# Merge products of a four-branch decoder trunk: one fp32 product of two matmuls, or three passes over high and low parts

## The chip, the cores and the metric

The kernel runs on one core of a Trainium2 chip. The metric is the time of one execution on the device in microseconds (us), the median of three runs. In the text TensorE is PE (its weight loads PEld), VectorE is DVE, ScalarE is ACT, GpSimd is POOL and SyncE is SP, as in the profile.

## The reference, cut to what matters

Two layers. In each, the normalized activations `h` (512 tokens x 1024) meet one large input projection; its columns feed four mixers (A gated DeltaNet, "g" in the kernel; B latent attention, "m"; C RWKV-7, "r"; D top-k sparse attention, "d") and four gates of 1024 channels. Each mixer gives 256 features per token, which are projected to 1024, gated and summed:

```python
y_a = gdn_mixer(...)  @ w_out_gdn[l]      # (512 x 256) @ (256 x 1024)
y_b = mla_mixer(...)  @ w_out_mla[l]
y_c = rwkv7_mixer(...) @ w_out_rwkv[l]
y_d = dsa_mixer(...)  @ w_out_dsa[l]
merged = sigmoid(p_a) * y_a + sigmoid(p_b) * y_b + sigmoid(p_c) * y_c + sigmoid(p_d) * y_d
x = x + merged @ w_o[l]
hm = rms_norm(x, mlp_norm_g[l])
x = x + square(relu(hm @ w_up[l])) @ w_down[l]
```

Everything is float32. The change touches only the four `@ w_out` products.

## The kernel before, in words

Activations lie transposed: features on the 128 partitions, the 512 tokens along the free dimension. All large weight matrices are cut into units of 1024 x 128 (eight tiles of 128 x 128), 134 units a layer, streamed from one DRAM array in the order of `unit_list` (L59). A unit is loaded into one of three slots of `ring` by SP (L408 to L412, 512 KB). ACT then copies it into `w_hi` as fp32r, a reduced form of fp32 (`split_next`, L1178), and POOL subtracts to get the rest, `w_lo` (L446 to L452, two instructions of 128 x 512). `w_hi` and `w_lo` have two slots each, so a unit is split when the unit two before it has been consumed. The activations are held in the same two forms (`h_hi`, `h_lo`). PE makes the product in three passes, w_hi by h_hi, w_hi by h_lo, w_lo by h_hi: 24 matmuls of 128 x 512 a unit (`split_product`, L485, lines L491, L492 and L497).

A **merge unit** `("merge", br, i)` holds the gate weights of 128 of the 1024 channels of branch `br`, and behind them two tiles of 128 x 128 of that branch's outgoing matrix (128 KB). There are 32 a layer. PE makes the gate like any unit, into one of three PSUM banks that ACT empties (`bank_a`); ACT takes the sigmoid into one of four slots of `sg` and splits the next unit (`merge_sig`, L1147). `merge_outputs` (L561) then makes the outgoing product into one of four banks that DVE empties (`bank_v`): two plain fp32 matmuls, L567, whose operands are `out_ring` (the outgoing weights as loaded, six slots) and `yo` (the branch's 256 features, two slots of branches). The trace has two records for each fp32 matmul, so four for a product. DVE multiplies the product by the sigmoid and adds it to `mg` (`merge`, L1680: L1518 with output `sg`, then L1693; in branch 2, the first one, a single multiplication at L1689). Products are mostly made in pairs: two gates, then two products.

The order of every engine's work is written out by hand; each engine runs its own program in order, and semaphores join them. The order of a layer, with the branch numbers of the code (2 = RWKV, 0 = DeltaNet, 1 = latent attention, 3 = sparse attention):

1. Input projections and both recurrent mixers, with branch 2's merges between them. The RWKV features are made by DVE at L1889 and signalled by `r_out`; PE waits for it at L912, makes four products at once, then does two pairs (L930 and L938). Around there ACT takes two sets of inverse roots (L1354 and L1356), with table loads.
2. The DeltaNet features (L1940), then the projections of the sparse branch, then branch 0's eight merges (L985 to L1034), with the indexer's scores between them. DVE meanwhile adds up the scores (L1971) and runs a top-128 selection, cut into steps that `go_on` (L2004) takes from a generator: MAX8 (L1983), MATCH_REPLACE8 (L1985) and some steps behind them (L1989 to L1999).
3. Attention "m" (`attention`: L772 on PE, L1218 on ACT, L1697 on DVE). It works through 16 steps (4 query tiles x 4 heads), with the three first gates of branch 1 fed in as pieces (`gate_pieces`). ACT writes the attention's output into `yo` at L1237, eight pieces of 128 x 128, each one `m_y`.
4. Branch 1's merges: PE makes the fourth gate, waits for all eight `m_y` and makes four products, then two pairs. In the same stretch DVE runs the rest of the selection and the merges by turns (L2071 to L2079: attention, nine steps, two merges of two, eight steps, one merge, the last steps, one merge). Attention "d" needs the whole selection.
5. Attention "d" of the same form, branch 3's merges, then `wo`, `up` and `down`.

SP has one queue. For a merge unit it first loads the ring slot and then, behind a wait for `mg_done` (products merged by DVE), the outgoing weights (L413 to L417).

Of the kernel before, what the change touches and what calls it, by code (L numbers as in the profile page):

```python
# [16 lines left out]
ALU = mybir.AluOpType  # L17
ACT = mybir.ActivationFunctionType
F32 = mybir.dt.float32
# [25 lines left out]
INVERSE_STEPS = ("uc", "e", "x1", "ti", "y", "t", "x", "wt", "u")  # L45
# [7 lines left out]
OUT_RING = 6  # L53
# [113 lines left out]
def build(nc, x_in, pos_in, wstream, par_in, const_in, tabs, x_dram, out):  # L167
    ctx = ExitStack()
    with ctx:
        def sb(name, shape, dt=F32):  # L170
            return ctx.enter_context(nc.sbuf_tensor(name, shape, dt))
# [9 lines left out]
        out_ring = sb("out_ring", [P, OUT_RING, 2, P])  # L181
# [4 lines left out]
        yo = sb("yo", [P, 2, 2, T])  # L186
# [76 lines left out]
        for name, n in (  # L263
# [20 lines left out]
            ("m_ss", 16), ("m_p", 16), ("m_n", 16), ("m_pt", 16), ("m_y", 8),  # L284
            ("mg_sig", 32), ("mg_raw", 6), ("mg_done", 32), ("mg_hi", 8), ("mg_lo", 8), ("wo_done", 8), ("up_relu", 32), ("up_sq", 32), ("up_hi", 32), ("up_done", 32), ("g_zs", 1), ("r_s0", 1), ("g_s0", 1), ("down_done", 8 * QUARTERS),
# [54 lines left out]
        def merges_to(g):  # L340

            return sum(UNITS[i % NU][0] == "merge" for i in range(g))

        block = ctx.enter_context(nc.Block())
# [28 lines left out]
            tmp=ar(35, (T,)), ss=ar(11, (4, T)), pt=ar(15, (4, TT, P)),  # L373
# [4 lines left out]
            ss=ar(15, (4, T)), pt=ar(33, (4, TT, P)),  # L378
# [19 lines left out]
        def _(sp):  # L398
# [9 lines left out]
            for g in range(L * NU):  # L408
                l, u = divmod(g, NU)
                if g >= RING:  # L410
                    sp.wait_ge(S["split_lo"], g - RING + 1)
                sp.dma_start(ring[:, g % RING, :, :], wstream[g, :, 0:KT * P].rearrange("p (k n) -> p k n", n=P)).then_inc(w_here[g % RING], 16)  # L412
                if UNITS[u][0] == "merge":  # L413
                    n = merges_to(g)
                    if n >= OUT_RING:
                        sp.wait_ge(S["mg_done"], n - OUT_RING + 1)
                    sp.dma_start(out_ring[:, n % OUT_RING, :, :], wstream[g, :, KT * P:].rearrange("p (k n) -> p k n", n=P)).then_inc(out_here[n % OUT_RING], 16)  # L417
                if g == 0:
                    load_x(1)
                if g == 1:  # L420
                    sp.dma_start(consts[:, NFIRST:], const_in[:, NFIRST:]).then_inc(more_here, 16)
                if UNITS[u] == ("rw", 4):
                    if l == 0:
                        sp.wait_ge(S["x_t"], 8)
                    else:
                        sp.wait_ge(S["down_done"], at(l - 1, "down_done", 8 * QUARTERS))
                    sp.dma_start(x_dram, xT).then_inc(x_away, 16)
                if UNITS[u] == ("merge", 3, 0):
                    sp.wait_ge(S["m_y"], at(l, "m_y", 8))
                    sp.wait_ge(x_away, 16 * (l + 1))  # L430
                    sp.dma_start(xT, x_dram).then_inc(x_back, 16)
# [8 lines left out]
        def _(pool):  # L440
# [31 lines left out]
        def _(pe):  # L472
# [344 lines left out]
            for l in range(L):  # L817
# [94 lines left out]
                pe.wait_ge(S["r_out"], at(l, "r_out", 1))  # L912
# [72 lines left out]
                def indexed_merge(i):  # L985
                    numbers = []
                    for j in range(2):
                        numbers.append(gate(l, 0, 2 * i + j))
                        index_pair()
                    merge_outputs(1, numbers)  # L990
# [53 lines left out]
                pe.wait_ge(S["m_y"], at(l, "m_y", 8))  # L1044
# [10 lines left out]
                pe.wait_ge(S["d_y"], at(l, "d_y", 8))  # L1055
# [32 lines left out]
        def _(act):  # L1088
# [89 lines left out]
            def split_next():  # L1178


                g = units[0]
                if g < L * NU:
# [35 lines left out]
            def attention(l, x, V, slot, fill):  # L1218
                steps = [(qt, h) for qt in range(TT) for h in range(H)]
                for i in range(len(steps) + 3):  # L1220
# [12 lines left out]
                    if i >= 4 and i % 2 == 0:  # L1233
# [3 lines left out]
                        act_fn(yo[:, slot, h // 2, qt * P:(qt + 1) * P], b[:, 0:P], ACT.Copy).then_inc(S[x + "_y"], 1)  # L1237
# [33 lines left out]
            for l in range(L):  # L1271
# [173 lines left out]
                attention(l, "m", Mv, 0, lambda i: piecewise_sig(l, i))  # L1445
# [4 lines left out]
                attention(l, "d", Dv, 1, lambda i: piecewise_sig(l, i))  # L1450
# [50 lines left out]
        def _(dve):  # L1501
# [194 lines left out]

            def attention(l, x, V, scale, bias):  # L1697
                steps = [(qt, h) for qt in range(TT) for h in range(H)]
                scores = {}
                for i in range(len(steps) + 1):  # L1700
# [13 lines left out]
                    if i >= 1:  # L1714
# [5 lines left out]
                        v.tensor_scalar(e_, e_, att[:, 2, j % 4:j % 4 + 1], None, MUL).then_inc(S[x + "_n"], 1)  # L1720

# [35 lines left out]
            for l in range(L):  # L1757
# [472 lines left out]
```

## Time and profile before

| what | value |
|---|---|
| median of 3 runs | 2044.9 us (2044.44 to 2045.82) |
| the profiled execution's own time | 2043.76 us |
| its span | 2041.9 us |
| PE busy | 1987.6 us, 97% |
| DVE busy | 1087.1 us, 53% |
| ACT busy | 768.7 us, 38% |
| POOL busy | 737.3 us, 36% |
| granted TensorE clock, mean | 0.996 |

The span is the time from the first to the last instruction; the rest of the execution's time lies around it. A busy share is an average over the whole span. Each record of the trace belongs to a line of the kernel, and a helper's line stands for all its callers. Matmuls overlap, so that one's own duration is longer than the distance to the next; distances are read in the chain of waits, which goes back from the last instruction, at each step to what released it. What stands in square brackets behind an instruction of the timeline is the time its engine was idle before it, and what ended that.

### The profile page before, as it was taken

How to read it: one execution, taken by the hardware profiler on the slowest of the kernel's cores; microseconds unless marked ns; L12 is line 12 of the kernel's file. 1: busy time of each engine (PE TensorE's matmuls, PEld its weight loads, DVE VectorE, ACT ScalarE, POOL GpSimd, SP SyncE). 2: the span in 40 equal slices, each digit the busy share in tenths (PEclk: the TensorE clock that was granted, in tenths of full speed). 3: DMA queues.
4: the chain of work that ended last, by engine and by line, in shares of the span. 5: the costliest groups of instructions: out<-in, count | busy, mean ns of one | idle time of the engine just before them, and what ended most of it. 6: DMA issues, size and time to landing. Idle time of an engine off the chain costs nothing.

```text
span 2041.9 us, 31745 instructions
## 1 busy us (share of the span) xinstructions
PE 1987.6 (97%) x13120; PEld 1526.7 (75%) x13120; DVE 1087.1 (53%) x1807; ACT 768.7 (38%) x1206; POOL 737.3 (36%) x553
## 2 busy tenths in 40 slices
PE   6999999999999999999999999999999999999997
PEld 5788787756667888888867877776566778888886
DVE  8785555896833422222487756379876343222223
ACT  5442523344353442322354353234344433332323
POOL 3431313422324444444444132243213344444442
PEclk9999999999999999999999999999999999999999
DMA  6220112211312332333332111123122223233332
GB/s 231 75 81 28 57 34 78 84 59 50 122 55 77 114 102 93 95 101 93 97 121 90 47 37 58 43 79 95 52 78 81 68 85 101 93 101 95 94 102 73
DMA packets 51647, 169.42 MB, mean 83 GB/s; under 512 B 5728, under 2 KB 14048, under 8 KB 50864
## 3 DMA queue, kind: packets, MB, share of 16 engines
q1 hardware_dynamic: 50448, 163.11, 24.9%
q0 software_dynamic: 1056, 4.28, 0.6%
q8 instruction: 105, 1.72, 0.3%
q14 instruction: 38, 0.31, 0.0%
HBM read 160.29 MB, written 7.08 MB: 82 GB/s over the span
## 4 chain that ended last, share of the span: by engine, by line
PE 84%; DVE 11%; ACT 3%; issue 1%; DMA 0%; POOL 0%; ACTq 0%; SPq 0%; DVEq 0%
PE bank_a L491 13%; PE bank_a L497 13%; PE bank_a L492 13%; PE bank_v L497 7%; PE bank_v L491 7%; PE bank_v L492 7%; PE bank_v L567 4%; PE bank_v L645 3%; DVE arena L1518 1%; PE bank_a L804 1%; PE bank_f L599 1%; PE bank_f L605 1%; PE bank_f L578 1%; DVE mg L1524 1%; PE bank_a L793 1%
## 5 line engine op out<-in xcount | busy, mean ns | idle before, releaser
L451 POOL TENSOR_TENSOR w_lo<-ring,w_hi 128x512 fp32r<-128x512 f32 x536 | 729.6, 1382 | 1207.4 <-ACT w_hi L1184 1207.2
L491 PE MATMUL bank_a<-h_hi,w_hi 128*128 128x512 f32 x1296 | 523.8, 404 | 3.9 <-DVE h_lo L1557 3.9
L492 PE MATMUL bank_a<-h_lo,w_hi 128*128 128x512 f32 x1296 | 505.7, 390 | 0.0
L1184 ACT ACTIVATE w_hi<-ring 128x1024 fp32r<-128x1024 f32 x268 | 281.5, 1050 | 222.6 <-DVE arena L2118 212.4
L497 PE MATMUL bank_a<-h_hi,w_lo 128*128 128x512 f32 x1296 | 321.4, 390 | 0.0
L491 PEld LDWEIGHTS bank_a<-h_hi,w_hi 128*128 128x128 f32 x1296 | 243.4, 188 | 75.0 <-issue 19.4
L492 PEld LDWEIGHTS bank_a<-h_lo,w_hi 128*128 128x128 f32 x1296 | 243.6, 188 | 57.1 <-issue 8.1
L497 PEld LDWEIGHTS bank_a<-h_hi,w_lo 128*128 128x128 f32 x1296 | 244.0, 188 | 50.8
L491 PE MATMUL bank_v<-parts,w_hi 128*128 128x512 f32 x640 | 251.3, 393 | 1.4 <-DVE parts L2087 1.4
L492 PE MATMUL bank_v<-parts,w_hi 128*128 128x512 f32 x640 | 249.1, 389 | 0.0
L1518 DVE TENSOR_TENSOR sg<-bank_v,sg 128x512 f32<-128x512 f32 x112 | 77.4, 691 | 310.5 <-PE bank_v L497 239.3
L2106 DVE TENSOR_TENSOR arena<-arena 128x512 f32<-128x512 f32 x64 | 44.3, 692 | 244.7 <-ACT arena L1477 244.7
L497 PE MATMUL bank_v<-parts,w_lo 128*128 128x512 f32 x640 | 158.1, 389 | 0.0
L491 PEld LDWEIGHTS bank_v<-parts,w_hi 128*128 128x128 f32 x640 | 120.1, 188 | 29.0 <-DVE parts L2087 4.1
L497 PEld LDWEIGHTS bank_v<-parts,w_lo 128*128 128x128 f32 x640 | 120.1, 188 | 25.0
L492 PEld LDWEIGHTS bank_v<-parts,w_hi 128*128 128x128 f32 x640 | 120.2, 188 | 24.9 <-issue 0.5
L1477 ACT ACTIVATE arena<-bank_a 128x512 f32<-128x512 f32 x64 | 38.3, 598 | 205.6 <-PE bank_a L497 205.6
L567 PE MATMUL bank_v<-yo,out_ring 128*128 128x512 f32 x256 | 114.7, 594 | 0.0
L1154 ACT ACTIVATE sg<-bank_a 128x512 f32<-128x512 f32 x52 | 31.1, 597 | 202.1 <-PE bank_a L497 202.1
L1518 DVE TENSOR_TENSOR arena<-arena 128x512 f32<-128x512 f32 (+3 forms) x77 | 97.8, 1270 | 10.7 <-ACT arena L1247 8.2
L567 PEld LDWEIGHTS bank_v<-yo,out_ring 128*128 128x128 f32 x256 | 48.0, 189 | 54.5 <-issue 53.0
L645 PE MATMUL bank_v<-arena 64*64 64x64 f32 x2176 | 66.2, 219 | 3.1 <-ACT arena L1107 2.1
(296 smaller groups left out, 2505.5 us busy)
## 6 DMA issues: line engine op xcount, KB each, us to landing
ring<-in_w SPq DMA_DIRECT2D x268, 512.0 KB, 3.5
out_ring<-in_w SPq DMA_DIRECT2D x64, 128.0 KB, 3.4
x_dram<-arena SPq DMA_DIRECT2D x2, 2048.0 KB, 8.8
arena<-x_dram SPq DMA_DIRECT2D x2, 2048.0 KB, 9.1
arena<-in_x SPq DMA_DIRECT2D x2, 1024.0 KB, 9.4
out_x<-arena SPq DMA_DIRECT2D x4, 512.0 KB, 3.7
consts<-in_const SPq DMA_DIRECT2D x1, 1189.0 KB, 13.6
arena<-tabs POOLq DMA_DIRECT2D x2, 512.0 KB, 3.9
```

Source lines behind the costliest of these rows:

```text
L451: ins = nc.gpsimd.tensor_tensor(w_lo[:, g % SPLIT, ks, :], raw, w_hi[:, g % SPLIT, ks, :].bitcast(F32), ALU.subtract)
L491: mm(b[:], w_hi[:, s, k, :], hi[:, k, :], start=k == 0, stop=False)
L492: mm(b[:], w_hi[:, s, k, :], lo[:, k, :], start=False, stop=False)
L497: ins = mm(b[:], w_lo[:, s, k, :], hi[:, k, :], start=False, stop=k == KT - 1)
L567: ins = mm(b[:], out_ring[:, n % OUT_RING, k, :], yo[:, slot, k, :], start=k == 0, stop=k == 1)
L578: mm(b[:], hi[:, k, :], h_hi[:, k, :], start=k == 0, stop=False)
L645: ins = mm(b[quarter(p_), k * C:(k + 1) * C], lhs[quarter(p_), m, :], rhs(m, p_), start=True, stop=True)
L1154: act_fn(sg[:, n % GATES, :], b[:], ACT.Sigmoid).then_inc(S["mg_sig"], 1)
L1184: act_fn(w_hi[:, g % SPLIT, :, :], ring[:, g % RING, :, :], ACT.Copy).then_inc(S["split_hi"], 1)
L1477: act_fn(relu[:, n % 2, :], b[:], ACT.Relu).then_inc(S["up_relu"], 1)
L1518: link(v.tensor_tensor(out_, a, b, op))
L2106: v.tensor_tensor(relu2[:, n % 2, :], relu[:, n % 2, :], relu[:, n % 2, :], MUL).then_inc(S["up_sq"], 1)
```

## The change

The product of the outgoing weights becomes three passes over high and low parts, as for all other weights.

- **PE**, `merge_outputs`: six fp32r matmuls of 128 x 512 in place of two fp32 matmuls; it waits for `ow_lo` instead of the load.
- **Weights.** `out_ring`, `out_hi` and `out_lo` have four slots where `out_ring` had six. `out_ring` and `out_lo` share their bytes (the `with` block gives its space back, and `out_lo` is allocated next), so POOL subtracts in place, and a slot is loaded anew only when the product from it has been merged. For each pair of merge units, SP loads the outgoing weights of both at the unit behind the second gate, ACT makes two `out_hi` (128 x 256 each) and POOL two `out_lo` (128 x 256 each), each ahead of its own part of that unit's split. That split is done when the pair's first gate has been consumed. `outgoing(g)` gives the pair for unit g.
- **Features.** `yo` gives way to `y_hi` and `y_lo` of one branch. For r and g, DVE writes the features to the arena and then parts them, two copies and two subtractions of 128 x 512 (`parts_of`). In the attentions ACT copies each piece twice, into `y_hi` and into `yt`, and DVE subtracts in four instructions of 128 x 256 (`low_rows`), three inside the loop, from step 8, and one behind it.
- **Waits.** PE waits for `r_yl`, `g_yl`, `m_yl`, `d_yl` where it waited for the features. DVE waits in `low_rows` for ACT's `m_y` and `d_y`.

```diff
-OUT_RING = 6
+OUT_RING = 4
...
-        out_ring = sb("out_ring", [P, OUT_RING, 2, P])
+        out_hi = sb("out_hi", [P, OUT_RING, 2, P], F32R)
+        with nc.sbuf_tensor("out_ring", [P, OUT_RING, 2, P], F32) as out_ring:
+            pass
+        out_lo = sb("out_lo", [P, OUT_RING, 2, P], F32R)
...
+        def outgoing(g):
+
+            if not 0 < g < L * NU or UNITS[(g - 1) % NU][0] != "merge" or merges_to(g - 1) % 2 == 0:
+                return []
+            second = merges_to(g - 1)
+            first_owner = max(i for i in range(g - 1) if UNITS[i % NU][0] == "merge")
+            return [(second - 1, first_owner), (second, g - 1)]
...
-                if UNITS[u][0] == "merge":
-                    n = merges_to(g)
+                for n, owner in outgoing(g):
                     if n >= OUT_RING:
                         sp.wait_ge(S["mg_done"], n - OUT_RING + 1)
-                    sp.dma_start(out_ring[:, n % OUT_RING, :, :], wstream[g, :, KT * P:]...
+                    sp.dma_start(out_ring[:, n % OUT_RING, :, :], wstream[owner, :, KT * P:]...
...
+                for n, owner in outgoing(g):
+                    pool.wait_ge(S["ow_hi"], n + 1)
+                    slot = n % OUT_RING
+                    nc.gpsimd.tensor_tensor(out_lo[:, slot, :, :], out_ring[:, slot, :, :], out_hi[:, slot, :, :].bitcast(F32), ALU.subtract).then_inc(S["ow_lo"], 1)
                 pool.wait_ge(S["split_hi"], g + 1)
...
-                    pe.wait_ge(out_here[n % OUT_RING], 16 * (n // OUT_RING + 1))
+                    pe.wait_ge(S["ow_lo"], n + 1)
+                    hi, lo = out_hi[:, n % OUT_RING], out_lo[:, n % OUT_RING]
                     for k in range(2):
-                        ins = mm(b[:], out_ring[:, n % OUT_RING, k, :], yo[:, slot, k, :], start=k == 0, stop=k == 1)
+                        mm(b[:], hi[:, k, :], y_hi[:, k, :], start=k == 0, stop=False)
+                        mm(b[:], hi[:, k, :], y_lo[:, k, :], start=False, stop=False)
+                    for k in range(2):
+                        ins = mm(b[:], lo[:, k, :], y_hi[:, k, :], start=False, stop=k == 1)
...
                 g = units[0]
+                for n, owner in outgoing(g):
+                    if n >= OUT_RING:
+                        act.wait_ge(S["mg_done"], n - OUT_RING + 1)
+                    act.wait_ge(out_here[n % OUT_RING], 16 * (n // OUT_RING + 1))
+                    act_fn(out_hi[:, n % OUT_RING, :, :], out_ring[:, n % OUT_RING, :, :], ACT.Copy).then_inc(S["ow_hi"], 1)
...
-                        act_fn(yo[:, slot, h // 2, qt * P:(qt + 1) * P], b[:, 0:P], ACT.Copy).then_inc(S[x + "_y"], 1)
+                        rows = slice(qt * P, (qt + 1) * P)
+                        act_fn(y_hi[:, h // 2, rows], b[:, 0:P], ACT.Copy)
+                        act_fn(V["yt"][:, h // 2, rows], b[:, 0:P], ACT.Copy).then_inc(S[x + "_y"], 1)
...
+            def parts_of(l, x, src):
+
+                for f in range(2):
+                    link(v.tensor_copy(y_hi[:, f, :], src[:, f, :]))
+                    v.tensor_tensor(y_lo[:, f, :], src[:, f, :], y_hi[:, f, :].bitcast(F32), SUB).then_inc(S[x + "_yl"], 1)
+
+            def low_rows(l, x, V, qt):
+
+                rows = slice(qt * P, (qt + 1) * P)
+                dve.wait_ge(S[x + "_y"], at(l, x + "_y", 2 * qt + 2))
+                v.tensor_tensor(y_lo[:, :, rows], V["yt"][:, :, rows], y_hi[:, :, rows].bitcast(F32), SUB).then_inc(S[x + "_yl"], 1)
...
+                    if i >= 8 and i % 4 == 0:
+                        low_rows(l, x, V, i // 4 - 2)
+                low_rows(l, x, V, TT - 1)
...
-                v.tensor_tensor(yo[:, 0, :, :], R["o"], R["g"], MUL).then_inc(S["r_out"], 1)
+                v.tensor_tensor(R["o"], R["o"], R["g"], MUL).then_inc(S["r_out"], 1)
                 dve.wait_ge(S["r_out"], reached("r_out"))
+                parts_of(l, "r", R["o"])
...
-                v.tensor_tensor(yo[:, 1, :, :], G["o"], G["z"], MUL).then_inc(S["g_out"], 1)
+                v.tensor_tensor(G["o"], G["o"], G["z"], MUL).then_inc(S["g_out"], 1)
                 dve.wait_ge(S["g_out"], reached("g_out"))
+                parts_of(l, "g", G["o"])
```

## Rows read from the trace of the kernel before

**Rows 1.** The page, part 4: the chain of waits by engine.
```profile
PE 84%; DVE 11%; ACT 3%; issue 1%; DMA 0%; POOL 0%; ACTq 0%; SPq 0%; DVEq 0%
```

**Rows 2.** Chain of waits behind attention d: start, us, what.
```profile
604.52 1.81 PE bank_a L497 x8
609.96 1.81 PE bank_a L497 x8
611.77 3.43 PE bank_v L567 x8
...
626.13 1.73 PE bank_v L567 x4
627.89 0.70 DVE sg L1518
```

**Rows 3.** Stretches (start:end, length; PE, PEld, DVE, ACT, POOL busy; clock, DMA).
```profile
376.00:471.00 95.00, 95.00 (x345) 58.49 (x343) 89.46 (x164) 35.86 (x53) 28.75 (x21) 1.00 0.23 72
471.00:509.00 38.00, 35.61 (x215) 25.00 (x216) 21.36 (x74) 19.97 (x59) 5.08 (x5) 1.00 0.16 50
509.00:552.00 43.00, 43.00 (x168) 29.62 (x164) 39.24 (x66) 13.67 (x18) 16.35 (x12) 1.00 0.37 128
```

**Rows 4.** Timeline of DVE in branch 0's merges.
```profile
396.49 2.87 DVE L1971 SCALAR_TENSOR_TENSOR arena<-arena,ab 128x384 f32<-128x384 f32 x2 [0.26 <-ACT arena L1396]
...
403.00 2.87 DVE L1971 SCALAR_TENSOR_TENSOR arena<-arena,ab 128x384 f32<-128x384 f32 x2 [0.22 <-ACT arena L1396]
...
414.11 0.43 DVE L1518 TENSOR_TENSOR arena<-arena 128x256 f32<-128x256 f32 x1
...
429.10 3.03 DVE L1971 SCALAR_TENSOR_TENSOR arena<-arena,ab 128x512 f32<-128x512 f32 x2 [0.41 <-ACT arena L1396]
```

**Rows 5.** DVE and POOL together, and DVE alone.
```profile
462.54 2.98 POOL L451 TENSOR_TENSOR w_lo<-ring,w_hi 128x512 fp32r<-128x512 f32 x2 [24.27 <-ACT w_hi L1184]
...
464.41 1.66 DVE L2068 TENSOR_TENSOR arena<-arena 32x512 f32<-32x512 f32 x1
...
467.54 0.68 DVE L2068 TENSOR_TENSOR arena<-arena 32x512 f32<-32x512 f32 x1
```

**Rows 6.** Timeline of DVE behind attention m, layer 0, and the same wait in layer 1.
```profile
503.68 0.41 DVE L1521 TENSOR_SCALAR arena<-arena,m 128x384 f32<-128x384 f32 x1
...
517.39 0.69 DVE L1518 TENSOR_TENSOR sg<-bank_v,sg 128x512 f32<-128x512 f32 x1
...
548.99 0.69 DVE L1518 TENSOR_TENSOR sg<-bank_v,sg 128x512 f32<-128x512 f32 x1 [2.02 <-PE bank_v L567]
...
552.38 0.29 DVE L1711 CUSTOM_DVE_ANT_0 arena<-bank_v,consts 128x128 f32<-128x128 f32 x1
...
1506.15 0.41 DVE L1521 TENSOR_SCALAR arena<-arena,m 128x384 f32<-128x384 f32 x1
...
1551.47 0.69 DVE L1518 TENSOR_TENSOR sg<-bank_v,sg 128x512 f32<-128x512 f32 x1 [2.01 <-PE bank_v L567]
```

**Rows 7.** Timeline of ACT in attention m and its end, layer 0 and layer 1.
```profile
481.29 0.28 ACT L1237 ACTIVATE yo<-bank_a 128x128 f32<-128x128 f32 x1 [0.62 <-PE bank_a L804]
481.47 0.59 ACT L1165 ACTIVATE sg<-bank_f 128x512 f32<-128x512 f32 x1
...
509.41 0.28 ACT L1237 ACTIVATE yo<-bank_a 128x128 f32<-128x128 f32 x1 [2.29 <-PE bank_a L804]
...
1511.89 0.28 ACT L1237 ACTIVATE yo<-bank_a 128x128 f32<-128x128 f32 x1 [2.29 <-PE bank_a L804]
```

**Rows 8.** Timeline of PE in attention m.
```profile
482.20 0.47 PE L599 MATMUL bank_f<-h_hi,w_hi 128*128 128x512 f32 x1 [0.58 <-ACT sg L1165]
```

**Rows 9.** Chain of waits around the RWKV features.
```profile
209.57 0.94 ACT w_hi L1184
210.53 1.28 ACT L1245
211.83 0.70 ACT arena L1245
212.57 1.13 PE bank_a L770 x2
```

**Rows 10.** Groups of ACT by shape: busy, mean ns; idle before.
```profile
L1184 ACT ACTIVATE w_hi<-ring 128x1024 fp32r<-128x1024 f32 x268 | 281.5, 1050 | 222.6 <-DVE arena L2118 212.4 <-PE bank_v L848 10.1
L1216 ACT ACTIVATE h_hi<-mg 128x512 fp32r<-128x512 f32 x16 | 9.7, 626 | 0.4
```

**Rows 11.** Timeline of ACT between the DeltaNet's pair matrices.
```profile
255.35 1.09 ACT L1120 ACTIVATE arena<-bank_a 128x512 f32<-128x512 f32 x2 [0.19 <-PE bank_a L620]
```

**Rows 12.** Timeline of DVE behind the RWKV features and the DeltaNet features.
```profile
220.99 0.69 DVE L1689 TENSOR_TENSOR mg<-bank_v,sg 128x512 f32<-128x512 f32 x1 [4.93 <-PE bank_v L567]
...
336.70 0.69 DVE L1518 TENSOR_TENSOR arena<-bank_v,arena 128x512 f32<-128x512 f32 x1 [0.58 <-PE bank_v L970]
...
343.05 0.69 DVE L1518 TENSOR_TENSOR arena<-bank_v,arena 128x512 f32<-128x512 f32 x1 [2.12 <-PE bank_v L970]
```

**Rows 13.** The page, part 6: issues, KB each, us to landing.
```profile
out_ring<-in_w SPq DMA_DIRECT2D x64, 128.0 KB, 3.4
```

More of the change, by code:

```diff
@@ L44 @@
 BLOCK = 8
-INVERSE_STEPS = ("uc", "e", "x1", "ti", "y", "t", "x", "wt", "u")
+INVERSE_STEPS = ("yl", "uc", "e", "x1", "ti", "y", "t", "x", "wt", "u")
 GDN0, MLA0, RWK0, DSA0, GATE0 = 0, 1032, 1448, 2472, 3824
@@ L185, in build @@
         par = sb("par", [P, NPAR])
-        yo = sb("yo", [P, 2, 2, T])
+        y_hi = sb("y_hi", [P, 2, T], F32R)
+        y_lo = sb("y_lo", [P, 2, T], F32R)
         misc = sb("misc", [P, 2, T])
@@ L284, in build @@
             ("m_ss", 16), ("m_p", 16), ("m_n", 16), ("m_pt", 16), ("m_y", 8),
+            ("r_yl", 2), ("g_yl", 2), ("m_yl", 4), ("d_yl", 4), ("ow_hi", 32), ("ow_lo", 32),
             ("mg_sig", 32), ("mg_raw", 6), ("mg_done", 32), ("mg_hi", 8), ("mg_lo", 8), ("wo_done", 8), ("up_relu", 32), ("up_sq", 32), ("up_hi", 32), ("up_done", 32), ("g_zs", 1), ("r_s0", 1), ("g_s0", 1), ("down_done", 8 * QUARTERS),
@@ L372, in build @@
             iq=ar(15, (4, T)), q=ar(19, (2, T)), k=ar(21, (2, T)), vf=ar(23, (2, T)), v=ar(25, (TT, 256)), tab=ar(27, (2, T)), ik=ar(29, (T,)),
-            tmp=ar(35, (T,)), ss=ar(11, (4, T)), pt=ar(15, (4, TT, P)),
+            tmp=ar(35, (T,)), ss=ar(11, (4, T)), pt=ar(15, (4, TT, P)), yt=ar(27, (2, T)),
         )
@@ L377, in build @@
             tab=ar(27, (2, T)), tmp=ar(29, (T,)), bias=ar(32, (T,)), kr=ar(33, (T,)),
-            ss=ar(15, (4, T)), pt=ar(33, (4, TT, P)),
+            ss=ar(15, (4, T)), pt=ar(33, (4, TT, P)), yt=ar(27, (2, T)),
         )
@@ L911, in _ @@
                 more.append(gate(l, 2, 3))
-                pe.wait_ge(S["r_out"], at(l, "r_out", 1))
+                pe.wait_ge(S["r_yl"], at(l, "r_yl", 2))
                 merge_outputs(0, numbers)
@@ L989, in indexed_merge @@
                         index_pair()
+                    pe.wait_ge(S["g_yl"], at(l, "g_yl", 2))
                     merge_outputs(1, numbers)
@@ L1043, in _ @@
                 numbers.append(gate(l, 1, 3))
-                pe.wait_ge(S["m_y"], at(l, "m_y", 8))
+                pe.wait_ge(S["m_yl"], at(l, "m_yl", 4))
                 merge_outputs(0, numbers)
@@ L1054, in _ @@
                 numbers.append(gate(l, 3, 3))
-                pe.wait_ge(S["d_y"], at(l, "d_y", 8))
+                pe.wait_ge(S["d_yl"], at(l, "d_yl", 4))
                 merge_outputs(1, numbers)
@@ L1216, in norm_root, with attention @@
                         act_fn(h_hi[:, k, :], mg[:, k, :], ACT.Copy).then_inc(S["n_hi"], 1)
-            def attention(l, x, V, slot, fill):
+            def attention(l, x, V, fill):
                 steps = [(qt, h) for qt in range(TT) for h in range(H)]
@@ L1444, in _ @@
                 merge_sig(l)
-                attention(l, "m", Mv, 0, lambda i: piecewise_sig(l, i))
+                attention(l, "m", Mv, lambda i: piecewise_sig(l, i))
                 late_sig(l, 3)
@@ L1449, in _ @@
                 merge_sig(l)
-                attention(l, "d", Dv, 1, lambda i: piecewise_sig(l, i))
+                attention(l, "d", Dv, lambda i: piecewise_sig(l, i))
                 late_sig(l, 6)
```

2 lines of the change are left out of this document (1 added, 1 removed).

## The prediction

> **What bounds the kernel now.** I read the busy shares first: PE is at 97%, and that is an average. The chain of waits gives the ends: 84% PE, 11% DVE, 3% ACT [rows 1]. So a microsecond off PE is a microsecond off the time only where the chain runs through PE. Three stretches decide this change, and for them I read the stretches' busy times and then each engine's timeline.
>
> In branch 0's merges, from 376 us to the start of attention m, PE is busy for the whole 95 us, but DVE is too, 89.5 of 95 [rows 3]; what is missing is mostly the small gaps between its short instructions. DVE waits for other work only three times behind the first product, 0.26, 0.22 and 0.41 us, 0.89 together [rows 4]. From 429 us to 472 us it doesn't wait at all, and the next attention starts when it is through. In attention m DVE has room (21.4 of 38 us) and PE leads (35.6) [rows 3]. In branch 1's merges PE is again busy throughout and DVE 39.2 of 43 [rows 3]: DVE starts on the selection at 503.68, and its only wait before attention d is 2.02 us, for the first product of the last pair [rows 6]. Layer 1 shows the same 2.01. Behind attention d, and around branch 2, PE leads.
>
> **What a product gains.** A unit of 24 fp32r matmuls comes every 5.44 us (604.52 to 609.96), and eight of them take 1.81 us, so one takes 0.227 us [rows 2]. Two fp32 products take 3.43 us, one 1.717 [rows 2]. Six fp32r matmuls take 6 x 0.227 = 1.36 us. PE is relieved of 0.357 us a product, 22.8 us over 64. Bounds for the new matmul: the same kind of operands and the same changing of weights in each unit gives 0.227; the nearest dearer row is half an fp32 matmul, 0.429, which would make the product dearer than before. I take 0.227, since `split_product` has the same three passes.
>
> **Branch 2 (per layer).** Eight products on the path give 8 x 0.357 = 2.86 us. Two costs stand against it. ACT makes two `out_hi` ahead of a `w_hi`. No row shows a copy of 128 x 256 into fp32r; 128 x 1024 takes 1.05 us and 128 x 512 0.63 [rows 10], so the straight line gives 0.41, and the next instruction begins some 0.1 us before an end (0.94 in the chain for 1.05) [rows 9, 10]: 0.32 each, 0.65 a pair. Bounds are 0.43 (half of 0.63 less the overlap, twice) and 1.06 (0.63 less the overlap, twice). The pair of gates 2 and 3 falls at 209.57, where the chain runs through ACT: w_hi, table load, logarithm, then PE's matmuls that wait for its bank [rows 9]. That is +0.65 in full. The pair of gates 6 and 7 falls ahead of the copies at 255.35, where ACT had waited only 0.19 for PE [rows 11], and PE waits for these copies' banks: +0.46. Net 1.75 us gained. The parting of the features by DVE (two copies, two subtractions; 0.69 us or less each by the 128 x 512 rows, 2.8 together) is hidden: DVE idled 4.93 us ahead of the first product it merges [rows 12], and PE reaches `r_yl` later than DVE does. Without that cover it would be 2.8. The same for g lies ahead of waits of 0.58 and 2.12 us [rows 12], and its products come 50 us later: nothing, 0.1 us if only the first two waits counted.
>
> **Branch 0.** Eight products, but DVE leads: of 2.86 us only its own waits can go, 0.89. Late next is DVE itself. Here POOL's new work counts: four pairs, two subtractions of 128 x 256 each. Half of POOL's 2.98 for two of 128 x 512 is 1.49 for one [rows 5], so about 0.75 for a new one, 1.5 a pair. Beside POOL a DVE instruction with two inputs in SBUF takes 1.66 us instead of 0.68, 0.98 more for a POOL instruction of 1.49 [rows 5]; for one of 0.75 that is 0.5, or 1.0 a pair. Bounds: 0 if all fall on other instructions (half of DVE's work there is MAX8 and MATCH_REPLACE8), 4.0 for all four. I take 1.5, since two pairs fall on the rotary and elementwise parts. Net 0.6 us lost.
>
> The Trainium skill, "SBUF — State Buffer", section "Who interferes with whom", says that a VectorE instruction with two SBUF inputs contends with a GpSimd one that reads SBUF, and that the later one is blocked until the other ends. By the rows above the trace agrees. It is the rule that speaks against this change, and the dear end below is it at its worst.
>
> **Attentions m and d.** ACT copies each output piece twice; the second copy moves what is behind it by 0.18 us (481.29 to 481.47) [rows 7]. Twice in an attention what stands behind is the emptying of `bank_f`, for which PE waits (0.58 us) [rows 7, 8]: 0.36 us. The first pair's `out_hi` (0.65) delays an exponential whose result PE needs two steps later; DVE's three `low_rows` in the loop (0.43 each by the 128 x 256 row [rows 4]) fall into its idle time. Bounds 0 and 8 x 0.18 + 0.65 = 2.1 each; I take 0.5 each, 1.0 together.
>
> **Behind attention m: the term that decides.** The last `low_rows` of attention m waits for all eight pieces, and stands on DVE ahead of the rest of the selection. DVE was through with the attention at 503.68, the last piece is begun by ACT at 509.41 [rows 6, 7]. With the second copy it is there at 509.41 + 0.18 + 0.28 = 509.87; 0.43 for the subtraction, and DVE goes on at 510.3, 6.6 us later. Queued behind it are all selection steps and the eight merges of branch 1, and attention d waits for these. DVE had 2.02 us of idle time to take this up [rows 6], so attention d starts 4.6 us later, and the PE time of branch 1's eight products gives nothing, since PE then has to wait for DVE. Layer 1 has the same distance, 1511.89 to 1506.15 [rows 6, 7].
>
> The load of the third pair now waits until 18 products are merged. DVE starts merging at 517.39 + 6.6 = 524.0 [rows 6] and has two done by about 527.9; 3.4 us to landing [rows 13], 0.65 on ACT and about 1.4 on POOL let PE start that pair at 533.4, some 2 us late. The last pair is then ready before 550, and DVE comes for it at 553.6: hidden, by 4 us. Behind attention d the same wait of DVE costs nothing, because it has only merges to do there.
>
> **Branch 3.** PE leads: seven products give 2.5 us; the last is covered by DVE, which needs longer for a product than PE (it begins to merge at 627.89, and the second product isn't on the chain [rows 2]). 2.4 us with a little lost at the end.
>
> **Sum per layer:** -1.75 (branch 2), +0.6 (branch 0), +1.0 (attentions), +4.6 (wait behind attention m), -2.4 (branch 3) = +2.05; over two layers +4.1 us. The profiled execution took 2043.76 us (2.0 less in the span), so it would take 2047.9; the median of the runs is 1.1 above it, so the forecast is 2049.0.
>
> **Rivals.**
> - *Faster: DVE's wait is covered.* If DVE had more than 6.6 us idle between the attentions, the wait would vanish, and its 2.02 us could be gained as well: per layer -1.75 + 0.6 + 1.0 - 2.0 - 2.4 = -4.6, together -9.1, 2035.8 us. For it: PE is busy there without a gap. Against it: 2.02 us is all that the timeline shows.
> - *No difference that counts: the small costs hide.* ACT's copies and POOL's subtractions find room: -2.86 - 0.89 + 4.6 - 2.5 = -1.65 a layer, 2041.6 us. For it: ACT is busy for 20 of 38 us in the attention and POOL for 5 [rows 3].
> - *Clearly slower: the new POOL and ACT work falls on DVE's and PE's path.* All four pairs of branch 0 at 1.0 instead of 1.5 in all (+2.5), and each attention 0.8 dearer (+1.6): +4.1 a layer more, 2057 us. It decides from two-input DVE instructions beside every pair on. For it: rows 5. Against it: much of DVE's work there has one input.
> - *The passes aren't at 0.227 us.* Then PE gains nothing or loses. Nothing in the trace speaks for it.
>
> **How the numbers follow.** Forecast 0.50, covered wait 0.13, small costs hidden 0.17, POOL and ACT dear 0.17, passes dear 0.03. What a measurement of this kernel can tell from no change is about 0.2%, 4.1 us, so from 2040.8 to 2049.0 counts as the same. The forecast sits on that edge and is halved. Slower: 0.25 + 0.17 + 0.03 = 0.45. Same: 0.25 + 0.14 = 0.39. Faster: 0.13 + 0.03 = 0.16. The range, 2041 to 2057, holds the forecast, the hidden and the dear case; the forecast's own is 2045 to 2053.
>
> **What would show it.** Six records of 0.227 us distance a product. DVE idle for about 5.7 us ahead of its first instruction behind attention m, released by ACT's copy, and no wait left before attention d, which starts some 4.6 us later relative to attention m's end. The stretch from branch 0's first product to attention m as long as before or slightly longer. `up` and `down` unchanged. The forecast is wrong if DVE resumes the selection near the time it did, if attention d starts earlier, or if PE waits for `ow_lo` pair by pair.

## The result, and the profile after

| | before | after |
|---|---|---|
| median | 2043.86 us (20 runs) | 2047.25 us (20 runs) |
| profiled execution, its span | 2043.76, 2041.9 us | 2047.01, 2045.2 us |
| granted clock of that execution, mean | 0.996 | 0.992 |

The ratio is 1.0018, with a 95% interval of 1.0011 to 1.0025: 3.7 us more, clear of the noise, and just inside what the prediction counted as no difference. The medians are 3.4 us apart. One of the 20 executions of after took 10981.48 us; it is left out of the ratio, and without it the median is 2047.01. The forecast was 2049.0.

The page of after, parts 1 and 4: PE has 15 us less to do, POOL 55 and ACT 25 more, and part of the chain that ended last has moved from PE (84% [rows 1], now 76%) to DVE (11%, now 19%).

```profile
PE 1972.5 (96%) x13248; PEld 1553.6 (76%) x13248; DVE 1109.9 (54%) x1839; ACT 794.2 (39%) x1302; POOL 792.8 (39%) x617
...
PE 76%; DVE 19%; ACT 3%; issue 1%; DMA 0%; POOL 0%; ACTq 0%; SPq 0%; DVEq 0%
```

The chain of waits of after in branch 3, which answers to [rows 2] (start, us, what). A product is six distances of 0.23, 1.40 us in all (613.06 less 611.66), where it was 1.72.

```profile
609.85 1.81 PE bank_a L513 x8
611.66 0.23 PE bank_v L584
611.89 0.23 PE bank_v L585
612.13 0.23 PE bank_v L584
612.36 0.23 PE bank_v L585
612.59 0.47 PE bank_v L587 x2
613.06 0.23 PE bank_v L584
```

DVE's timeline of after behind attention m, layer 0 and 1, for [rows 6]. The subtraction waits for ACT; the selection follows at 506.28, where DVE began at 503.68 although attention m now ended 4 us earlier. In front of attention d there is no wait left.

```profile
499.89 0.42 DVE L1735 TENSOR_TENSOR y_lo<-arena,y_hi 128x256 fp32r<-128x256 f32 x1
505.94 0.42 DVE L1735 TENSOR_TENSOR y_lo<-arena,y_hi 128x256 fp32r<-128x256 f32 x1 [5.63 <-ACT arena L1265]
506.28 0.41 DVE L1549 TENSOR_SCALAR arena<-arena,m 128x384 f32<-128x384 f32 x1
...
549.21 0.69 DVE L1546 TENSOR_TENSOR sg<-bank_v,sg 128x512 f32<-128x512 f32 x1
...
552.11 0.29 DVE L1751 CUSTOM_DVE_ANT_0 arena<-bank_v,consts 128x128 f32<-128x128 f32 x1
...
1512.19 0.43 DVE L1735 TENSOR_TENSOR y_lo<-arena,y_hi 128x256 fp32r<-128x256 f32 x1 [5.63 <-ACT arena L1265]
```

PE's timeline of after, at the end of the same stretch and ahead of layer 1's inverse roots: what DVE lost is now PE's idle time.

```profile
552.23 0.55 PE L804 MATMUL bank_v<-arena 64*128 64x128 f32 x1 [6.59 <-DVE mg L1721]
...
1214.92 2.07 PE L790 MATMUL bank_a<-arena,consts 128*128 128x512 f32 x2 [2.26 <-ACT arena L1273]
```

Stretches of after, columns as in [rows 3], the granted clock third from the end. Behind either idle time it falls; in the kernel before it is 1.00 in the same places.

```profile
548.00:550.00 2.00, 0.00 (x0) 0.00 (x0) 1.87 (x4) 0.00 (x0) 0.00 (x0) 0.78 0.22 88
550.00:552.00 2.00, 0.00 (x0) 0.00 (x0) 1.93 (x3) 0.00 (x0) 0.00 (x0) 0.50 0.14 36
552.00:554.00 2.00, 1.19 (x6) 0.96 (x7) 1.55 (x12) 1.18 (x5) 0.00 (x0) 0.50 0.32 99
554.00:556.00 2.00, 2.00 (x7) 1.51 (x6) 0.68 (x5) 0.80 (x5) 0.00 (x0) 0.52 0.00 0
...
1212.00:1216.00 4.00, 1.74 (x4) 0.56 (x3) 3.93 (x3) 3.97 (x5) 4.00 (x3) 0.84 0.08 28
1216.00:1220.00 4.00, 4.00 (x14) 2.84 (x13) 3.92 (x5) 2.96 (x4) 1.77 (x2) 0.74 0.00 0
```

Where the time went, from the same instruction's start in both traces (after less before). Layer 0 opens 1.01 us ahead at the RWKV features, which is not the change: in the trace of before the clock fell to 0.50 at 44 us, behind 2.26 us of idle time of PE, and in the trace of after it did not, behind the same 2.26 (before, then after).

```profile
44.00:48.00 4.00, 3.83 (x10) 2.86 (x11) 3.76 (x9) 0.00 (x0) 0.00 (x0) 0.57 0.39 131
...
44.00:48.00 4.00, 3.68 (x16) 2.85 (x16) 3.77 (x8) 0.48 (x1) 0.00 (x0) 1.00 0.37 131
```

| stretch | forecast | layer 0 | layer 1 |
|---|---|---|---|
| branch 2 | -1.75 | -1.95 | -0.4 |
| branch 0 | +0.6 | -1.35 | -1.0 |
| attention m | +0.5 | +0.35 | +2.0 |
| wait and branch 1 | +4.6 | +3.7 | +3.7 |
| attention d | +0.5 | +1.45 | } -0.2 |
| branch 3 | -2.4 | -1.95 | } |
| sum | +2.05 | +0.25 | +4.1 |

### The profile page after: what moved, and what is told of

It is laid out like the page before. It is cut to its first block, busy times and chain, and to the rows that moved or that the text cites. A ratio compares the mean times of both kernels' runs of the same rounds, so it can differ in the third digit from the quotient of the medians.

```text
span 2045.2 us, 32253 instructions
## 1 busy us (share of the span) xinstructions
PE 1972.5 (96%) x13248; PEld 1553.6 (76%) x13248; DVE 1109.9 (54%) x1839; ACT 794.2 (39%) x1302; POOL 792.8 (39%) x617
## 3 DMA queue, kind: packets, MB, share of 16 engines
q8 instruction: 106, 1.74, 0.3%
## 4 chain that ended last, share of the span: by engine, by line
PE 76%; DVE 19%; ACT 3%; issue 1%; DMA 0%; POOL 0%; ACTq 0%; SPq 0%; DVEq 0%
PE bank_a L507 11%; PE bank_a L513 11%; PE bank_a L508 11%; PE bank_v L513 7%; PE bank_v L507 7%; PE bank_v L508 7%; PE bank_v L665 3%; DVE arena L2030 3%; DVE m L2028 3%; DVE arena L1546 2%; DVE arena L2016 2%; DVE mg L1721 1%; DVE sg L1546 1%; PE bank_f L619 1%; PE bank_a L824 1%
## 5 line engine op out<-in xcount | busy, mean ns | idle before, releaser
L507 PEld LDWEIGHTS bank_a<-h_hi,w_hi 128*128 128x128 f32 x1296 | 243.6, 188 | 72.7 <-issue 16.7
L462 POOL TENSOR_TENSOR out_lo<-out_ring,out_hi 128x256 fp32r<-128x256 f32 x64 | 55.7, 890 | 297.5 <-ACT out_hi L1207 297.5
L665 PEld LDWEIGHTS bank_v<-arena 64*64 64x64 f32 x2176 | 64.9, 135 | 3.5 <-ACT arena L1128 2.8
```

The lines of the kernel that those rows point to most:

```text
L462: nc.gpsimd.tensor_tensor(out_lo[:, slot, :, :], out_ring[:, slot, :, :], out_hi[:, slot, :, :].bitcast(F32), ALU.subtract).then_inc(S["ow ...
L507: mm(b[:], w_hi[:, s, k, :], hi[:, k, :], start=k == 0, stop=False)
L665: ins = mm(b[quarter(p_), k * C:(k + 1) * C], lhs[quarter(p_), m, :], rhs(m, p_), start=True, stop=True)
```

## The experiments

Each was timed in five rounds beside the kernel before. The first four shared a chip (before: 2043.24 us there), so did the next four (2043.87) and the last two (2043.04). Between groups, and against the changed kernel, the ratios to before are the safer comparison; differences of medians are given with them. A trace is of one execution, which can lie some us from the median. `before_wait` and `before_steps` start from the kernel before, the others from the changed kernel.

### low_split: the last subtraction behind four selection steps

```diff
-                low_rows(l, x, V, TT - 1)
+                if x != "m":
+                    low_rows(l, x, V, TT - 1)
...
-                go_on(9)
+                go_on(4)
+                low_rows(l, "m", Mv, TT - 1)
+                go_on(5)
```

> The changed kernel, with one thing moved: attention m's last low_rows (the subtraction that waits for ACT's last copy) stands behind four steps of the selection instead of ahead of them. Theory (the wait in front of the queued selection costs 3.7 us a layer by the trace, and PE's idle 6.6 us ahead of attention d another 1 us by a clock of 0.5 behind it): DVE starts on the selection without a wait, its wait for ACT shrinks to under 1 us, the next attention starts some 4 to 5 us earlier in each layer, and the time falls by 8 to 10 us against the changed kernel, to 2037 to 2039 us, 5 to 7 us under the kernel before. Rival (the wait is covered by other idle time, and what the change costs is ACT's and POOL's new work): within 2 us of the changed kernel, about 2047 us.

2036.14 us, ratio to before 0.9968 (0.9957 to 0.9979): 11.1 us under the changed kernel by the medians, 10.2 by the two ratios, at or a little above the upper end of what was expected, and the sign of the whole change turns. DVE's timeline:

```profile
498.96 0.42 DVE L1735 TENSOR_TENSOR y_lo<-arena,y_hi 128x256 fp32r<-128x256 f32 x1
499.29 0.41 DVE L1549 TENSOR_SCALAR arena<-arena,m 128x384 f32<-128x384 f32 x1
...
505.41 0.43 DVE L1735 TENSOR_TENSOR y_lo<-arena,y_hi 128x256 fp32r<-128x256 f32 x1
```

The subtraction comes behind the fourth step and waits for nothing. Attention d starts at 546.77 instead of 552.11; 1.0 us of this was there before branch 0, and 4.4 are the move. In layer 1 the two traces move 6.1 us apart, 1.6 of them because the clock did not fall at attention m's start this time. DVE still has no wait in branch 1, and PE idles ahead of attention d: DVE is the bound of this stretch now.

```profile
546.88 0.34 PE L804 MATMUL bank_v<-arena 64*128 64x128 f32 x1 [2.19 <-DVE mg L1721]
```

### before_wait: the wait alone, in the kernel before

```diff
                 attention(l, "m", Mv, 96 ** -0.5, lambda qt: Mv["bias"][:, (3 - qt) * P:T])
+                dve.wait_ge(S["m_y"], at(l, "m_y", 8))
```

> The kernel before, with one wait added: DVE waits for the eighth m_y (ACT's last copy of attention m) ahead of the selection. Nothing else of the change is in it. Theory (this wait alone costs, in any kernel with this order): DVE resumes 6.0 to 6.1 us later (509.41 + 0.28 against 503.68), 2.0 of it is taken up by its idle time, so 4 us a layer, and up to 1 us for the clock behind PE's new idle time: 2052 to 2054 us. Rival (the wait is hidden, and the changed kernel's loss comes from its other new work): 2044 to 2045 us, as the kernel before.

2058.61 us, ratio 1.0073 (1.0060 to 1.0086): 15.4 us (15 by the ratio), half as much again as expected. The mechanism stands, its price was too low. DVE's timeline shows the wait as expected, and behind it two instructions of 0.62 and 0.56 us (128 x 384) that take 1.74 and 1.54:

```profile
509.13 0.42 DVE L1521 TENSOR_SCALAR arena<-arena,m 128x384 f32<-128x384 f32 x1 [5.96 <-ACT yo L1237]
509.59 0.96 DVE L1994 TENSOR_TENSOR_SCAN arena<-arena 128x384 f32<-128x384 f32 x1
510.59 1.74 DVE L1524 SCALAR_TENSOR_TENSOR arena<-arena,sml 128x384 f32<-128x384 f32 x1
512.36 1.54 DVE L1518 TENSOR_TENSOR arena<-arena 128x384 f32<-128x384 f32 x1
```

Moved by 6 us, the selection's two-input steps meet POOL's subtractions. By the offsets of the two traces in layer 0 the wait costs 6.0 us, these two 2.1, the steps up to 545.58 another 0.7, and 3.4 are taken up before attention d (2.0 of them DVE's old idle time), so that attention d starts 5.4 late, in layer 1 too. Attention d itself is 2.2 us longer in layer 0 and 1.7 in layer 1, with the clock at 0.50 behind PE's 5.71 us of idle time; that term was expected at 1 us at most. Together this is 14.6 us. Another 1.4 us lie in layer 1's recurrent stretch, ahead of the wait, and have no cause shown here.

### two_pass: the third pass left out

```diff
-                        mm(b[:], hi[:, k, :], y_lo[:, k, :], start=False, stop=False)
-                    for k in range(2):
-                        ins = mm(b[:], lo[:, k, :], y_hi[:, k, :], start=False, stop=k == 1)
+                        ins = mm(b[:], hi[:, k, :], y_lo[:, k, :], start=False, stop=k == 1)
```

> The changed kernel without the third pass of the outgoing product (low part of the weights by high part of the features is left out of the result): four matmuls of 0.234 us instead of six. All weights are still loaded and parted and all waits are kept. Theory (PE's time per product counts in branches 2 and 3 alone, where PE leads; in branch 0 and branch 1 DVE leads): 15 products a layer by 0.47 us, 7.0 us a layer, 14 us in all, to 2033 us, with at most 2 us more. Rival (PE's time counts in all 32 products of a layer): 30 us, to 2017 us. Rival (the passes hide in other waits): under 5 us.

2036.53 us, ratio 0.9963 (0.9949 to 0.9976): 10.7 us under the changed kernel by the medians, 10.2 by the ratios: less than the 14, or 12 at the least, of the theory, and far from 30. In layer 0, branches 2 and 3 give 2.5 and 2.3 us behind their first product and 0.5 for that one, 5.8 together. Branch 1 gives 0.6 us a layer and branch 0 nothing: the trace is 0.53 us ahead of the changed kernel's behind the last merges of branch 2, and 0.31 behind it at the start of attention m. What is missing goes along with the clock. PE now idles 2.47 us inside branch 0 (0.48 in the changed kernel) and 2.06 ahead of attention m (1.17); the clock fell behind the first in both layers and behind the second in layer 0, and the execution's mean clock is 0.988. In this kernel relieving PE where DVE leads bought idle time, and a lower clock came with it.

### low_split_roots: the pair's copies behind the inverse roots

```diff
-                for n, owner in outgoing(g):
-                    ...
+                if g >= L * NU or UNITS[g % NU] != ("merge", 2, 4):
+                    outgoing_hi(g)
...
                 inverse_roots(G["rs"], ...)
+                outgoing_hi(l * NU + UNITS.index(("merge", 2, 4)))
```

> The changed kernel with the last low_rows of attention m moved as in low_split, and the two out_hi of branch 2's second pair made behind the inverse roots of the DeltaNet instead of ahead of w_hi. Theory (two copies of 0.61 us in all stand on the chain ahead of the roots, and in layer 1 they lengthen PE's idle time from 1.65 to 2.26 us, behind which the clock falls): 0.5 us a layer and about 1 us of clock in layer 1, so 1.5 to 2.5 us under low_split. Rival (PE is the bound there and catches up, or the copies come just as late for POOL and PE): within 0.5 us of low_split.

2036.53 us, ratio 0.9962 (0.9950 to 0.9975), no difference from low_split. Yet PE's idle time at the roots went back from 2.27 to 1.66 us and the clock stayed at 1.00 there in both layers. In layer 1 DVE's first merge came at 1218.79, 1.1 us ahead of low_split; behind the start of attention m this was gone, where the clock fell (0.74 and 0.83 between 1466 and 1474) behind 1.17 us of idle time. In low_split the same idle time had left it at 1.00. Inconclusive by itself, so it was repeated on a better base below.

### steps_inside: selection steps into attention m's idle time

```diff
-                go_on(9)
+                go_on(8)
...
-                attention(l, "m", Mv, 96 ** -0.5, lambda qt: Mv["bias"][:, (3 - qt) * P:T])
-                go_on(4)
-                low_rows(l, "m", Mv, TT - 1)
-                go_on(5)
+                attention(l, "m", Mv, 96 ** -0.5, lambda qt: Mv["bias"][:, (3 - qt) * P:T],
+                          lambda i: go_on(1) if i in (8, 12, 14) else None)
+                go_on(2)
+                low_rows(l, "m", Mv, TT - 1)
+                go_on(7)
```

> low_split with three selection steps moved into attention m, where DVE has idle time (3.2, 2.7 and 3.3 us ahead of the scores of steps 8, 12 and 14): one of the nine in front of attention m and two from behind it. Theory (since the change DVE is the bound in branch 0 and branch 1, and PE's idle time ahead of an attention, 1.18 us for m and 2.19 us for d, costs itself and then a fallen clock): attention m starts 1.2 us earlier, attention d another 2.2 us, and the clock behind attention d's start stays at 1.00 (0.8 us more): 3.4 to 4.2 us a layer, to 2028 to 2030 us. Rival (DVE's steps delay attention m itself, or PE becomes the bound at once): 0 to 2 us in all, 2034 to 2036 us.

2033.11 us (2029.61 to 2037.08), ratio 0.9951 (0.9939 to 0.9963): 3 us under low_split (3.5 by the ratios) where 6 to 8 were expected. The trace is of an execution of 2036.69 us, in which the clock fell at layer 0's roots, at layer 1's attention m and at both attentions d. The moved steps cost attention m nothing, but two of them had covered ACT: DVE waits 2.79 us for the last copy again. PE's rows ahead of the attentions:

```profile
468.42 0.46 PE L804 MATMUL bank_v<-arena 96*128 96x128 f32 x2 [1.18 <-DVE mg L1721]
...
547.88 0.34 PE L804 MATMUL bank_v<-arena 64*128 64x128 f32 x1 [1.26 <-DVE mg L1721]
```

1.18 us ahead of attention m is what it was, though the last pair's first merge came 1.1 us earlier than in low_split and attention m started 0.7 us earlier. PE makes a product in 1.40 us and DVE merges one in 1.45 at best, so at the end of a pair DVE still has a merge to do, and PE waits for the bank. Here the additions to `mg` took 1.28 and 0.93 us, beside POOL, where 0.69 is the undisturbed time: 0.83 of the 1.18 us. That this is the whole of it is argued and not tested. The expectation that this idle time would go was wrong.

### steps_inside_roots

The two edits together.

> steps_inside, with the two out_hi of branch 2's second pair behind the inverse roots, as in low_split_roots, which gained nothing over low_split: at the roots the clock stayed at 1.00 in both layers, but it fell at the start of attention m in layer 1 behind 1.17 us of idle time. Theory (the gain at the roots was real, 0.5 us and once 1 us of clock, and was lost to that fall): with no idle time ahead of attention m it shows, 1 to 2 us under steps_inside. Rival (the copies only change place): within 0.5 us of steps_inside.

2031.10 us, ratio 0.9937 (0.9925 to 0.9948), 2.0 us under steps_inside as the theory had it. The intervals of the two ratios overlap, and the executions of steps_inside alone lie 7.5 us apart, so it is likely and not settled.

### busy_pe: useless work for PE

```diff
-                    for k in range(2):
-                        ...
+                    for _ in range(1 + again * (n == numbers[-1])):
+                        ...
...
-                    merge(l, 1, 0, i)
+                    merge(l, 1, 0, i, again=i == 3)
```

> low_split with useless work: in branch 1 the last product's six matmuls are done twice in each layer (1.4 us more for PE), in the 2.19 us in which PE idles ahead of attention d. Theory (the clock falls behind an idle time of 2.17 us and more, and did not behind 1.65 us or less ahead of the roots): PE's idle time is 0.8 us, the clock stays at 1.00 at attention d's start, and the kernel becomes 0.8 to 0.9 us a layer shorter through more work, 2034.5 us. Rival (the fall has another cause, or the repeat delays DVE's last merge, for which it has 0.9 us to spare): equal to low_split or up to 1 us a layer longer.

2035.58 us, ratio 0.9963 (0.9950 to 0.9975), 0.6 us under low_split (1.0 by the ratios) and within its interval. PE idles 0.76 us instead of 2.19; in layer 1 the clock stayed at 1.00, in layer 0 it fell to 0.66 all the same. Inconclusive.

### double_pool: POOL's new work twice

```diff
                 pool.wait_ge(S["split_hi"], g + 1)
+                for n, owner in outgoing(g):
+                    nc.gpsimd.tensor_tensor(w_lo[:, g % SPLIT, 0:2, :], ring[:, g % RING, 0:2, :], w_hi[:, g % SPLIT, 0:2, :].bitcast(F32), ALU.subtract).then_inc(S["ow_lo"], 1)
+                    pool.wait_ge(S["ow_lo"], 4 * (n // 2) + 3 + n % 2)
```

> low_split with POOL's new work doubled: for each outgoing weight tile POOL subtracts another 128 x 256 (0.9 us), behind out_lo, into the part of w_lo that its next instruction writes. This doubles what the change put on POOL beside DVE, and delays w_lo by 1.8 us at 16 units a layer. Theory (POOL's subtractions cost DVE little, since most of DVE's work beside them has one input): under 1 us a layer, 2036 to 2038 us. Rival (each of the POOL subtractions holds a two-input DVE instruction of the selection stretch or of a merge; where DVE leads, seven pairs a layer by 0.5 to 1.0 us): 3.5 to 7 us a layer, 2043 to 2050 us.

2039.09 us, ratio 0.9979 (0.9970 to 0.9987): 3.0 us over low_split by the medians, 2.2 by the ratios, whose intervals overlap: 1.1 to 1.5 a layer, between the two expectations. POOL's and DVE's timelines in front of attention m:

```profile
457.94 2.33 POOL L465 TENSOR_TENSOR w_lo<-ring,w_hi 128x256 fp32r<-128x256 f32 x2
460.34 6.35 POOL L470 TENSOR_TENSOR w_lo<-ring,w_hi 128x512 fp32r<-128x512 f32 x4
```

```profile
460.43 1.75 DVE L1549 TENSOR_TENSOR arena<-arena 32x512 f32<-32x512 f32 x1
462.21 1.66 DVE L2117 TENSOR_TENSOR arena<-arena 32x512 f32<-32x512 f32 x1
```

DVE runs the same 164 instructions in layer 0 from 376 us of before to the start of attention m. Their durations add up to 90.65 us in the kernel before, 89.86 in the changed one, 89.88 in low_split and 90.72 here; the idle time between them is 5.57, 5.03, 5.03 and 5.42 us. Layer 1 has the same order (91.16, 90.34, 90.26, 91.23). So the change's own pairs cost DVE nothing in sum, since other instructions than before met POOL, and doubling them cost 0.8 us and 0.4 of idle time. The rest of the loss isn't the lock alone: behind 1.76 us of idle time ahead of attention m, 1.18 in low_split, the clock fell in both layers here and in neither there, 1.6 us each, and branch 1 gave 1.0 of them back.

### best, and before_steps

`best` is steps_inside_roots with the wait covered:

```diff
-                go_on(2)
+                go_on(4)
                 low_rows(l, "m", Mv, TT - 1)
-                go_on(7)
+                go_on(5)
```

> steps_inside_roots with attention m's last low_rows behind four selection steps instead of two. There DVE waited 2.79 us for ACT's last copy, and PE idled 1.26 us ahead of attention d. Theory (what DVE loses there ahead of attention d comes back until the last product of branch 1 decides): DVE's wait goes, PE idles 0.8 us or less ahead of attention d, 0.5 to 1.3 us a layer, to 2029 to 2030 us. Rival (PE is the bound there already, and the 1.26 us are DVE's merge behind the last product): within 0.5 us of 2031.1.

2030.59 us (2028.08 to 2031.39), ratio 0.9935 (0.9923 to 0.9948). DVE's wait for ACT is gone, and it waits for the product instead:

```profile
541.48 0.69 DVE L1552 TENSOR_TENSOR sg<-bank_v,sg 128x512 f32<-128x512 f32 x1 [3.55 <-PE bank_v L587]
```

PE is the bound of branch 1 again. The 2.79 us brought 0.5 by the medians and nothing that can be told by the ratios (0.9935 and 0.9937), the rival's answer: they had been covered. PE still idles 0.99 us ahead of attention d. The trace is of the fastest of the five executions, and its chain has less DVE than before the change [rows 1]:

```profile
PE 88%; DVE 7%; ACT 3%; issue 1%; DMA 0%; POOL 0%; ACTq 0%; SPq 0%; DVEq 0%
```

This is the lowest median, 12.5 us under the kernel before and 16.7 under the changed one; from steps_inside_roots it can't be told apart.

`before_steps` puts the same three steps inside attention m of the kernel before.

> The kernel before, with the same three selection steps inside attention m as in steps_inside (one from in front, two from behind), and nothing else. Theory (before the change PE is busy without a gap in branch 0 and branch 1, so earlier selection steps give nothing; they pay only once the three passes have made DVE the bound): 2042 to 2044.5 us, no difference that can be measured. Rival (the selection steps pay in any kernel, and the change isn't needed for it): 3 to 6 us faster, 2038 to 2041 us.

2043.29 us, ratio 1.0000 (0.9991 to 1.0009). So `best` isn't a better order of the selection with the change thrown in: without the three passes these steps give nothing, and the three passes as first placed cost 3.7 us.

## Why the prediction was right, point by point

**The deciding term** was forecast from two rows and held: DVE resumes 6.55 us later relative to the attention's end, 6.6 forecast. low_split removes it and the gain appears; before_wait adds it alone and the loss appears. 3.7 us a layer instead of 4.6 reached attention d, because DVE and POOL met less in sum: the 75 instructions of DVE from its return to the selection up to attention d took 0.86 us less than before. Three at the start took 1.7 us more; of those that took less, two in the last steps of the selection (before, then after):

```profile
543.88 1.67 DVE L1518 TENSOR_TENSOR arena<-arena 128x512 f32<-128x512 f32 x1
545.58 1.40 DVE L1998 TENSOR_SCALAR arena<-arena 128x512 f32<-128x512 f32 x1
...
548.02 0.69 DVE L1546 TENSOR_TENSOR arena<-arena 128x512 f32<-128x512 f32 x1
548.75 0.43 DVE L2043 TENSOR_SCALAR arena<-arena 128x512 f32<-128x512 f32 x1
```

In before_wait the same 75 took 1.33 us more. A wait's price depends on what it pushes the queue into, by 0.9 us down and by 1.3 up in these two kernels, and the forecast had no term for this. The shorter ring of outgoing weights was forecast to cost nothing ahead of attention d, and PE has no idle time over 0.3 us there in the changed kernel before the 6.59.

**The clock** was missing from the forecast altogether. Attention d is 1.45 us longer, not 0.5. About 0.9 of it lies in the slow stretch, in which matmuls stand 0.43 us apart instead of 0.23. In layer 1 the clock also fell at the roots (about 1.5 us) and at attention m's start (about 1.6 us, behind 1.18 us of idle time), which are the +2.0 and the missing part of branch 2 in the table. None of these places had a fallen clock before.

**Branch 2.** -1.95 for -1.75 in layer 0. The first pair's copies took 0.61 us on the chain (0.65 forecast; one is 413 ns). The 0.46 for the second pair did not appear. A product gained 0.31 us, not 0.357, since a matmul came every 0.234 us.

**Branch 0** had the wrong sign, -1.35 measured for +0.6. The step that failed is POOL's 1.5 us: the forecast counted the pairs that the new subtractions would hold, and not those that would come apart when everything ahead ran 3 us earlier. The same 164 instructions of DVE took 0.79 us less in sum, not 1.5 more: the two at 396.49 [rows 4], for one, took 2.87 us and now 2.41, while the one at 412.27 took 0.48 and now, at 408.19, 1.33. The idle time between them fell by 0.54, waits of more than 0.2 us from 0.89 to 0.28 as forecast. The two make up the 1.35 us. "As long as before or slightly longer", one of the signs that the prediction named for this stretch, didn't come true.

**Branch 3.** -1.95 for -2.4: seven products at 0.31 are 2.2. **Feature parting** stayed hidden, though the first copy and the first subtraction took 1.38 and 1.67 us beside POOL at 212.52 and 213.94, and not 0.69 or less.

**What was luck.** Over both layers, branch 0 and branch 1 were forecast 5.4 us too dear, and about 4.9 us of clock (0.9 twice, 1.5 and 1.6) weren't forecast. The median came within 1.8 us of the forecast partly because these cancel. The forecast also started from a median of 2044.9 us, and 20 executions give 2043.86: as a difference it said +4.1, where 3.4 to 3.7 were measured.

POOL held instructions of one input too. DVE's and POOL's timelines of low_split, 1.55 us where 0.43 is the undisturbed time:

```profile
542.03 1.55 DVE L2044 TENSOR_SCALAR arena<-arena 128x512 f32<-128x512 f32 x1
```

```profile
542.01 2.72 POOL L467 TENSOR_TENSOR w_lo<-ring,w_hi 128x512 fp32r<-128x512 f32 x2 [0.56 <-ACT w_hi L1210]
```

The prediction had counted one-input work as safe, though the trace of before has the same instruction at 1.40 us, above. The Trainium skill, "SBUF — State Buffer", section "Who interferes with whom", says that copies, casts and `tensor_scalar` can enter modes in which VectorE takes the pair it shares with GpSimd. By this row the trace agrees.

## What to carry to other kernels

When a step gets a new input, look at what is queued behind it on its engine: here one subtraction of 0.43 us a layer, placed ahead of other work instead of four steps into it, cost 10 to 11 us, more than the 7 that the change gains without that wait. Before an engine is relieved, look which engine comes next in every stretch: where it is close, the gain turns into idle time, and the second engine has to be relieved in the same move. And put a price on the idle time itself: behind it the clock can fall. A count of the instructions that two engines will hold for each other isn't a price either; what moves apart counts with it.

## What the runs showed of the hardware

**A fallen clock after short idle times, and not every time.** From the 12 profiled executions, one case per layer:

| place | PE's idle time, us | clock below 1.00 |
|---|---|---|
| opening of layer 0, 44 us | 2.26 to 2.29 | 8 of 12 |
| roots | 1.65 to 1.67 | 0 of 12 |
| roots | 2.26 to 2.28 | 6 of 12, in one layer of each |
| attention m's start | 0.51 to 0.64 | 0 of 6 |
| attention m's start | 1.17, 1.18 | 6 of 14 |
| attention m's start | 1.76, 2.06 | 3 of 4 |
| attention d's start | 0.33, 0.34 | 0 of 4 |
| attention d's start | 0.76 to 1.26 | 5 of 10 |
| attention d's start | 2.17 to 2.19 | 4 of 4 |
| attention d's start | 5.71 to 7.37 | 6 of 6 |

The levels seen are 1.00 and 0.50, with mixtures where a stretch holds both. It can decide executions of one kernel: steps_inside ran in 2029.61 us at a mean clock of 0.996 and in 2037.08 at 0.992. The length of the idle time doesn't decide alone: 1.65 us at the roots never had a fall, 1.18 us ahead of attention m had one in 6 of 14. What selects the place, the layer or the execution isn't settled here, and that the idle time is the cause is argued from this table; busy_pe, which shortened one, was inconclusive. The kernel before has such falls too, at 44 us.

**The spread of the runs grew with the places where the clock may fall or not.** Before, 20 executions lie between 2041.69 and 2045.82 us. After, the 19 others lie between 2043.17 and 2051.47. Long idle time alone doesn't do it: before_wait, where PE idles 5.71 us ahead of attention d and the clock fell there in both layers of its trace, stays within 2.3 us in five executions, and steps_inside, with idle times of 1.17 to 2.28 us, spreads over 7.5. Five executions are few, and this is a reading, not a test.
